# Gate values of a recurrent mixer computed as rows inside the first norm stage

## The reference

```python
hp, hs = rms_norm(xp, g[0]), rms_norm(xs, g[0])
...
    qa, fa, ia, ga, qb, kb, vb, ob, gt = split_cols(h @ w_in, REC_COLS)
...
    gt = gt.astype(f32).reshape(B_, T, 2, H_B) + b_gates.astype(f32)
    ig, lf = gt[:, :, 0], jax.nn.log_sigmoid(gt[:, :, 1])
```

## Time and profile before

| | us |
|---|---|
| median of three runs | 4014.15 |
| lowest, highest | 4013.47, 4015.43 |
| the profiled execution | 4012.47 |
| its span | 4010.8 |
| TensorE busy | 3483.5 (87%) |
| VectorE (DVE) busy | 1918.7 (48%) |
| ScalarE (ACT) busy | 1150.3 (29%) |
| GpSimd (POOL) busy | 953.7 (24%) |

### The profile page before, as it was taken

The page is one execution under the profiler, slowest core; times in us unless marked ns, Lnnn a source line. Parts: engine busy times, 40 slices in busy tenths (PEclk is TensorE's granted clock), DMA queues, the critical chain, the costliest instruction groups (busy, mean ns, idle before and its releaser), DMA issues. The chain is left out here.

```text
span 4010.8 us, 52340 instructions
## 1 busy us (share of the span) xinstructions
PE 3483.5 (87%) x18274; PEld 2863.3 (71%) x18285; DVE 1918.7 (48%) x3316; ACT 1150.3 (29%) x2081; POOL 953.7 (24%) x918
## 2 busy tenths in 40 slices
PE   4889889885979999999799866885898699999998
PEld 4667666664779999888577723553366599999786
DVE  3145552123655455344445565799323655554344
ACT  2221222222511111143222144674254411111232
POOL 0000000000334443333111121121333243443332
PEclk9999999995989999999899765896898799999999
DMA  1111001101511111255221014363434311111454
GB/s 59 49 33 33 26 18 34 44 20 44 175 50 43 47 42 47 84 160 154 89 70 51 15 42 135 127 228 109 143 91 140 118 42 47 42 47 39 137 168 135
DMA packets 153899, 318.43 MB, mean 79 GB/s; under 512 B 22825, under 2 KB 73050, under 8 KB 153710
## 3 DMA queue, kind: packets, MB, share of 16 engines
q1 hardware_dynamic: 130414, 261.23, 20.7%
q0 software_dynamic: 16384, 44.06, 3.4%
q10 hardware_dynamic: 6912, 10.77, 0.8%
HBM read 287.49 MB, written 28.47 MB: 79 GB/s over the span
## 5 line engine op out<-in xcount | busy, mean ns | idle before, releaser
L57 PE MATMUL f_ps<-h,f_w 128*128 128x384 f32 (+1 forms) x2112 | 690.0, 327 | 27.2 <-POOL f_w L1270 27.2
L58 PE MATMUL f_ps<-h,f_w 128*128 128x384 f32 (+1 forms) x2112 | 687.9, 326 | 0.0
L59 PE MATMUL f_ps<-h,f_w 128*128 128x384 f32 (+1 forms) x2112 | 685.9, 325 | 0.0
L57 PEld LDWEIGHTS f_ps<-h,f_w 128*128 128x128 f32 x2112 | 398.0, 188 | 27.5 <-POOL f_w L1270 27.5
L58 PEld LDWEIGHTS f_ps<-h,f_w 128*128 128x128 f32 x2112 | 398.8, 189 | 0.0
L59 PEld LDWEIGHTS f_ps<-h,f_w 128*128 128x128 f32 x2112 | 398.4, 189 | 0.0
L1268 POOL TENSOR_TENSOR f_w<-f_w,f_one 128x1024 fp32r<-128x1024 f32 x88 | 210.8, 2396 | 577.2 <-PE f_ps L59 564.5
L387 DVE TENSOR_TENSOR d_w<-d_w 128x1024 fp32r<-128x1024 f32 x132 | 195.9, 1484 | 309.5 <-ACT d_w L326 308.5
L57 PE MATMUL d_psy<-d_w,d_l 128*128 128x512 f32 x792 | 310.9, 393 | 16.5 <-DVE d_w L387 16.5
L58 PE MATMUL d_psy<-d_w,d_l 128*128 128x512 f32 x792 | 310.0, 391 | 0.0
L59 PE MATMUL d_psy<-d_w,d_l 128*128 128x512 f32 x792 | 309.8, 391 | 0.0
(11 more groups left out here) (455 smaller groups left out, 6270.7 us busy)
## 6 DMA issues: line engine op xcount, KB each, us to landing
d_w<-in_w_down SPq DMA_DIRECT2D x132, 512.0 KB, 3.6
f_w<-in_w_up SPq DMA_DIRECT2D x88, 512.0 KB, 3.5
r_w<-in_w_rec SPq DMA_DIRECT2D x16, 1024.0 KB, 5.8
a_ring<-in_pool_ck POOLq DMA_DIRECT2D x64, 256.0 KB, 4.8
a_ring<-in_pool_ck SPq DMA_DIRECT2D x64, 256.0 KB, 4.4
a_ring<-in_pool_cv SPq DMA_DIRECT2D x64, 256.0 KB, 4.4
a_ring<-in_pool_cv POOLq DMA_DIRECT2D x64, 256.0 KB, 4.7
r_w<-in_w_out_rec SPq DMA_DIRECT2D x24, 512.0 KB, 3.7
```

Of the source, the lines that this page charges most:

```text
L57: pe.matmul(out, lhs[0], rhs[0], start=first, stop=False)
L58: pe.matmul(out, lhs[0], rhs[1], start=False, stop=False)
L59: return pe.matmul(out, lhs[1], rhs[0], start=False, stop=last)
```

## The change

The eight gate columns become the stationary operand, padded with zeros to 36 columns: the four input gates in columns 0 to 3, the four forget gates in columns 32 to 35, so that their results lie on partitions 0 to 3 and 32 to 35 of a PSUM tile that lives from the norm stage to the end of the gate stage. The activations move: three pieces of 384, 384 and 304 tokens, eight slices each. TensorE does these products inside the norm stage: the first piece behind the transposes of tile 3, the second behind those of tile 6, the third behind the last spread. The weights are loaded there by SP, ahead of tile 1, in two transfers of four columns for each of eight slices and 128 partitions, after DVE has cleared the tile. In the gate stage the products, the transposes and the copies go; ACT and DVE add the biases while they read PSUM, and the log sigmoid runs on four partitions of 1072 values instead of 128 partitions of 36.

```diff
 TG = 3
+GF = 32
...
-def norm_rows(nc, tag, const, x_in, gain, h_t):
+def norm_rows(nc, tag, const, x_in, gain, h_t, w_gates, gates):
...
+        wg = sb("wg", [P, KD, GF + H])
...
         @block.sync
...
                 if m == 1:
                     sp.dma_start(gn[:], gain).then_inc(gain_in, 16)
+                    sp.wait_ge(wg_zero, 1)
+                    with nc.allow_non_contiguous_dma(reason="eight gate columns"):
+                        sp.dma_start(wg[:, :, 0:H], w_gates[:, :, 0:H]).then_inc(wg_in, 16)
+                        sp.dma_start(wg[:, :, GF:GF + H], w_gates[:, :, H:2 * H]).then_inc(wg_in, 16)
...
         @block.tensor
         def _(pe):
+            def gate_products(c):
+                t0, tw = CH[c]
+                if c == 0:
+                    pe.wait_ge(wg_in, 32)
+                pe.wait_ge(h_done, TG * (c + 1))
+                for k in range(KD):
+                    mm = pe.matmul(gates[:, c, 0:tw], wg[:, k, :], h_t[:, k, t0:t0 + tw], start=(k == 0), stop=(k == KD - 1))
+                mm.then_inc(gates_done, 1)
+
             for m in range(NT):
...
                 t.then_inc(turned, 1)
+                if m % TG == 0 and m:
+                    gate_products(m // TG - 1)
+            gate_products(NT // TG - 1)
...
         @block.vector
         def _(dve):
+            nc.vector.memset(wg[:], 0.0).then_inc(wg_zero, 1)
             dve.wait_ge(gain_in, 16)
...
-def gate_rows(nc, const, h_t, w_gates, b_gates, m0, lb_logits, rows, cols, lb, one_lb, m_out):
+def gate_rows(nc, const, gates, b_gates, m0, lb_logits, rows, cols, lb, one_lb, m_out):
...
-            for dst, src in ((wg[:], w_gates), (bg[:], b_gates.partition_broadcast(P)), (m0s[:], m0), (lg[:], lb_logits)):
+            for dst, src in ((m0s[:], m0), (lg[:], lb_logits)):
                 sp.dma_start(dst, src).then_inc(loaded, 16)
+            with nc.allow_non_contiguous_dma(reason="eight gate biases"):
+                sp.dma_start(bg[:], b_gates.rearrange("(two h) -> h two", two=2)).then_inc(loaded, 16)
...
-            pe.wait_ge(loaded, 64)
-            for m in range(NT):
-                for k in range(KD):
-                    mm = pe.matmul(ps_g[0:rows_of(m), m, :], h_t[:, k, m * P:m * P + rows_of(m)], wg[:, k, :],
-                                   start=(k == 0), stop=(k == KD - 1))
-            mm.then_inc(gates_done, 1)
-            pe.wait_ge(lf_done, 1)
-            for m in range(NT):
-                r = rows_of(m)
-                for kind, src in ((0, gc[0:r, m, 0:H]), (1, lfc[0:r, m, :])):
-                    t = pe.transpose(ps_r[:, kind, m // 4, (m % 4) * P:(m % 4) * P + r], src, ident[0:r, 0:r])
-            t.then_inc(rows_done, 1)
...
         def _(act):
+            act.wait_ge(loaded, 48)
+            for t0, tw in CH:
+                c = t0 // CH[0][1]
+                nc.scalar.activation(fr[:, t0:t0 + tw], gates[GF:GF + H, c, 0:tw], ACT.Identity,
+                                     bias=bg[:, 1:2]).then_inc(f_out, 1)
...
-            dve.wait_ge(loaded, 64)
+            dve.wait_ge(loaded, 48)
+            for c, (t0, tw) in enumerate(CH):
+                link(nc.vector.tensor_scalar(ir[:, t0:t0 + tw], gates[0:H, c, 0:tw], bg[:, 0:1], None, ALU.add))
...
-            link(nc.vector.memset(gc[:], 0.0))
-            dve.wait_ge(gates_done, 1)
-            link(nc.vector.tensor_tensor(gc[:, 0:NT - 1, :], ps_g[:, 0:NT - 1, :],
-                                         bg[:].unsqueeze(1).to_broadcast([P, NT - 1, 2 * H]), ALU.add))
-            link(nc.vector.tensor_tensor(gc[0:LAST, NT - 1, :], ps_g[0:LAST, NT - 1, :], bg[0:LAST, :], ALU.add))
-            f = gc[:, :, H:2 * H]
-            nc.vector.scalar_tensor_tensor(out=ta[:], in0=f, scalar=-1.0, in1=f, op0=ALU.mult, op1=ALU.max).then_inc(abs_done, 1)
+            dve.wait_ge(f_out, len(CH))
+            nc.vector.scalar_tensor_tensor(out=ta[:], in0=fr[:], scalar=-1.0, in1=fr[:], op0=ALU.mult, op1=ALU.max).then_inc(abs_done, 1)
             dve.wait_ge(ln_done, 1)
-            nc.vector.scalar_tensor_tensor(out=lfc[:], in0=f, scalar=0.0, in1=ta[:], op0=ALU.min, op1=ALU.subtract).then_inc(lf_done, 1)
-            dve.wait_ge(rows_done, 1)
-            for kind, dst in ((0, ir), (1, lf)):
-                for c in range(3):
-                    w = min(512, T - c * 512)
-                    link(nc.vector.tensor_copy(dst[:, c * 512:c * 512 + w], ps_r[:, kind, c, 0:w]))
+            link(nc.vector.scalar_tensor_tensor(out=lf[:], in0=fr[:], scalar=0.0, in1=ta[:], op0=ALU.min, op1=ALU.subtract))
...
-        norm_rows(nc, "n0", const, a["x"], gain_c[0, 0], h_t)
+        gate_mem = ExitStack()
+        gates = gate_mem.enter_context(nc.psum_tensor("gates", [GF + H, len(CH), 512], F32))
+        norm_rows(nc, "n0", const, a["x"], gain_c[0, 0], h_t, a["w_gates"], gates)
```

More of the change, by code:

```diff
@@ L92, in norm_rows @@
         gn = sb("gn", [P, KD])
+        wg = sb("wg", [P, KD, GF + H])
         ps_t = ctx.enter_context(nc.psum_tensor(f"{tag}_pst", [P, 2, KD, P], F32))
+        wg_zero, wg_in = sem("wg_zero"), sem("wg_in")
         x_loaded = [sem(f"x_loaded{i}") for i in range(NX)]
         gain_in = sem("gain_in")
+        gates_done = sem("gates_done")
         sq_done = sem("sq_done")
@@ L459, in sem @@
             return used[-1]
-        wg = sb("wg", [P, KD, 2 * H])
-        bg = sb("bg", [P, 2 * H])
+        bg = sb("bg", [H, 2])
         m0s = sb("m0s", [H, DB])
@@ L465, in gate_rows @@
         lgx = sb("lgx", [P, 6, H])
[L466 to L469, removed]
+        fr = sb("fr", [H, T])
+        ta = sb("ta", [H, T])
+        te = sb("te", [H, T])
         ir = sb("ir", [H, T])
@@ L477, in gate_rows @@
         cs = sb("cs", [H, 3, T])
-        ps_g = ctx.enter_context(nc.psum_tensor("g_psg", [P, NT, 2 * H], F32))
-        ps_r = ctx.enter_context(nc.psum_tensor("g_psr", [H, 2, 3, 512], F32))
         ps_c = ctx.enter_context(nc.psum_tensor("g_psc", [P, NT, 3, H], F32))
[L481 to L484, removed]
+        loaded, f_out, abs_done, ln_done = (sem(x) for x in ("loaded", "f_out", "abs_done", "ln_done"))
+        expo_ready, rows_exp, cols_ready, cols_done = (
+            sem(x) for x in ("expo_ready", "rows_exp", "cols_ready", "cols_done"))
         cols_out, lb_sub, lb_exp, chain_s, stored, achain = (
@@ L536, in _ @@
             act.wait_ge(achain, 3)
-            nc.scalar.activation(te[:, 0, 0:1], ta[:, 0, 0:1], ACT.Copy).then_inc(rows_exp, 1)
+            nc.scalar.activation(te[:, 0:1], ta[:, 0:1], ACT.Copy).then_inc(rows_exp, 1)
         @block.vector
@@ L2683, in build @@
             lb, one_lb = sb(rt, "lb", [P, H]), sb(rt, "one_lb", [P, H])
-            gate_rows(nc, rc, h_t, a["w_gates"], a["b_gates"], a["m0"], a["lb_logits"], rows, cols, lb, one_lb,
+            gate_rows(nc, rc, gates, a["b_gates"], a["m0"], a["lb_logits"], rows, cols, lb, one_lb,
                       a["m_new"])
+            gate_mem.close()
             recurrent_mixers(nc, rc, h_t, mix_t, a["w_rec"], a["state_a"], a["state_b"], rows, cols, lb, one_lb,
```

## The result

The changed kernel takes **3992.7 us** (median of five runs, 3991.41 to 3995.79) against 4013.87 (five runs on the same chip, 4013.47 to 4015.43): a ratio of 0.9945 with a 95% interval of 0.9932 to 0.9959, 21 us faster. On a second chip the two stood at 3995.7 and 4019.83, ratio 0.9947 (0.9932 to 0.9962). The forecast was 4003.5 with a range of 3997.5 to 4011: the sign was right, the gain was twice the size foretold, outside the range.

The account below looks back on a forecast made before the run. The prediction took the norm and gate stages to be bound by one chain of engines waiting for each other. Its terms, -29.0 - 0.4 + 18.7 = -10.7 us, took the median from 4014.15 to 4003.5 us, range 3997.5 to 4011.

Parts of the forecast that it names:

- the norm stage, +18.7 foretold: Norm stage: small weight loads and three blocks of gate products make it end 18.7 us later than 35.93.
- Gate stage, -29.0: Gate stage: last landing to first scan takes 9.9 us instead of 38.9, a gain of 29.0 us.
- One issue fewer, -0.4: Gate stage: one DMA issue fewer ahead of the stage's last load saves 0.4 us.
- The loads, +1.5: Norm stage: two DMAs of 1024 16-byte pieces ahead of tile 1 delay it 1.5 us, bounds nothing and 4.4.
- The third rival: Norm-stage loads: small pieces worked off one after another cost 17.4 us instead of 1.5; net +5, 4019.5 us; chance 0.08.
- the estimate by its figure, 1.3 us on 16 engines: Norm-stage loads: about 10.5 ns a packet gives 1.3 us on 16 engines, leaving the sum where it is.
- I take 4.7 us to the rise: Norm stage, product blocks: TensorE's clock rises 4.7 us into a block, so a 384-column block costs 7.5 us.
- by then low again: Norm stage, tile 6's transposes: starting at 36.35, the clock is low again and they end at 38.3 us.
- I take 5.5: Norm stage, block three: the clock is about to fall, so 5.5 us, between 4.05 all high and 8.1 all low.
- the three sizes: Norm-stage clock assumptions: 4.7 us to the rise, low again by tile 6's transposes, 5.5 us for block three.
- The first rival: Norm stage: transposes keep the clock up between product blocks; net -15.4 us, 3998.8 us; chance 0.12.
- The second rival: Norm stage: the clock never rises in the product blocks; stage ends 28.6 us later, net -0.8, 4013.3 us; chance 0.10.

Follow-up runs that it names:

- number 6: Changed kernel with products tile by tile and 44 unread identity transposes ahead of tile 0, plus a one-column exponential on ACT before its wait, against that without it: 3987.86 us.
- number 7: The changed kernel profiled once more, with nothing changed: first mixer product at 99.07 us, norm stage end at 47.60 us.
- number 4: The kernel before the change with each tile's eight transposes made three times, against that kernel unaltered: 4018.71 us (one run).
- number 1: The changed kernel with its two weight loads issued ahead of tile 3 instead of tile 1: 3994.64 us, ratio 0.9947 to the kernel before.

## Why the prediction was wrong

The forecast named the right parts, and missed the size of one: the norm stage, +18.7 foretold, +12.35 measured.

- **Gate stage, -29.0: right.** 38.90 to 9.93 us, -28.97. The table load behind the pieces was counted rightly as the second step, though number 6 shows that it was worth only 0.5 us more than DVE's steps beside it, which the forecast put down as hidden.
- **One issue fewer, -0.4: right by luck.** The -0.44 between the norm's end and the last landing is -1.18 in the gate stage, where the term stood, and +0.74 ahead of it, of which the forecast had nothing. The former repeats (3.17 to 3.19 us before, 2.01 to 2.05 changed, in four profiles each): the term was three times as large as foretold.
- **The loads, +1.5: wrong.** 0.35 later in the profile, 0.14 in the means of four. The lower bound, nothing, was close to the answer: their issues took 0.68 and 0.66 us while tile 0 was still moving. The third rival falls with it. The Trainium skill (DMA: Bandwidth & Descriptors, Bandwidth) calls such transfers descriptor-dominated; the estimate by its figure, 1.3 us on 16 engines, can be true and hidden: these runs show only that next to nothing of it reached the path.
- **The clock, the step that failed.** "I take 4.7 us to the rise", "by then low again" for tile 6, and "I take 5.5" for block three were all too slow. Following the chain of after: tile 3 stands 1.65 us ahead of the working, of which 1.15 are the loads and 0.5 the landing of tile 4, explained below; block one takes 6.07 instead of 7.5 and ends 3.1 ahead; tile 6's transposes let block two start 1.05 us behind their own start instead of 1.97, 4.1 ahead; block two takes 6.97 instead of 7.5, 4.6 ahead; block three 4.28 instead of 5.85 with its hand-off, and the stage ends 6.3 us ahead. So some 4.6 us are the clock, 1.15 the loads and 0.5 that landing. It is no part of the clock: in the profile before, the squaring of tile 4 waited for it, and with it, in ACT's order, the scaling of tile 3:

```profile
18.41 1.06 ACT L134 ACTIVATE n_sq<-n_xt 128x1024 f32<-128x1024 f32 x1 [0.38 <-DMA n_xt<-in_x]
```

  In the profile after it didn't wait, and tile 3's transposes stand 2.17 us behind tile 2's (20.50 - 18.33) instead of 2.67. They do so in number 7 too (20.54 - 18.37), where tile 2's were low.
- **Why it failed:** the three sizes left out what transposes do for the clock. The evidence that they do nothing was one profile in which two groups of 1.97 us came in each 5.66 us and none rose. The absence of an event in one profile was read as a rule; number 4 shows that transposes raise the clock, and three further profiles of the same kernel show that they now and then do there. The first rival ("the clock stays up between the blocks", 0.12) had the mechanism. It was right on block three (4.28) in all four profiles, on tile 6 in three, and on block two in one (5.35). Idle time by itself doesn't decide that: the 2.82 us ahead of tile 6's transposes stand in all four. Nor does a run separate whether tile 4's and 5's transposes held the level up to tile 6, or it had simply not fallen yet, 4.7 us behind block one; in the profile that the forecast was read from it stayed up from 288.7 to 293.3, 4.6 us in which TensorE was busy for 1.53. That transposes raise the clock is shown, how much of the 4.6 us each of the two ways gives isn't.
- **The second rival,** a clock that never rises in the blocks, falls on block three alone: 4.28 us where the low level would take 8.1.
- **From the sum to the median.** Of the 10.8 us between 4003.5 and 3992.7, 6.6 lie ahead of the mixers, 2.5 behind them, and 1.7 are the distance from profile to median, which the changed kernel's profile did not have. The range's fast end, 3997.5, lay just below the first rival's 3998.8, and that rival came out 6.1 us slow as well: 1.9 ahead of the mixers, and the same 4.2 behind them and in the median.

## What to carry to other kernels

In this norm stage, where TensorE works in short groups with gaps, its clock level came from all it does there, transposes included. Before pricing new work in such a stage, ask what the old work and the new make together, and take more than one profile: three of four profiles of the kernel before show a rise that the fourth, from which the forecast was read, doesn't. Here the products gained the more the finer they were cut into the stage: the first mixer product came 12.5 us earlier with all of them at its end, 17.3 in three blocks and 24.6 tile by tile; waiting time used and a clock that stays up come together in that, and no run parts them. Taking a step off a chain is worth only its distance to the next row: the table load of 1.28 us gave back 0.5. And read from the trace whether an edit moved what it was to move: in number 1 the loads went behind two tiles in the program, and by 1 us in time.

## What the runs showed that was not expected

- Transposes, with no product near, raised the granted clock: 24 in 2.84 us instead of 5.9.
- Two loads of 1024 pieces of 16 bytes, issued while another transfer was moving, delayed the tile behind them by no more than its landing varies anyway: its squaring starts at 10.20 to 10.54 with them ahead and at 10.08 to 10.61 without them.
- Either kernel starts its mixers within 1.4 us in its four profiles, but the rest of its 3.9 ms differs by up to 14.2 us: the totals of a few runs say less about a change of this size than the mark at the end of the stage that it touches.
